# Two-layer encoder trunk on one core: the last four row blocks of the output projection kept back and multiplied token tile by token tile, with the second half's norm statistics taken from the additions' sums and a square pass

## The reference, cut to what matters

```python
branch = jnp.einsum('ble,ed->bld', y, w_out[i])          # 1024 x 2048 times 2048 x 1024
x = layer_norm(ALPHA * x + branch, ln_g[i], ln_b[i])     # mean and variance over 1024 features
```

## Time and profile before

| | us |
|---|---|
| three runs of before: median (lowest to highest) | 2169.07 (2167.77 to 2170.2) |
| the profiled execution, its own time | 2170.46 |
| its span, first to last instruction | 2168.6 |

### The profile page before, as it was taken

How to read it: one execution, slowest core, us unless ns; L and a number is a source line. 1 busy time by engine, 2 the same in 40 slices (tenths; PEclk the granted TensorE clock), 3 DMA queues, 4 the chain that set the end, 5 groups by cost and what they waited for, 6 DMA issues and landing times.

```text
span 2168.6 us, 31853 instructions
## 1 busy us (share of the span) xinstructions
PE 2107.2 (97%) x10880; PEld 1767.9 (82%) x10880; DVE 1628.4 (75%) x3673; ACT 1091.1 (50%) x2649; POOL 48.4 (2%) x65
## 2 busy tenths in 40 slices
PE   8999999999999995999999999999999999999996
PEld 8888888888888774888888888888888888888875
DVE  6777878787663568868888888888887888775485
ACT  5444444445553323455555555555555565564332
POOL 0000000000000021000000000000000000000031
PEclk9999999999999997999999999999999999999998
DMA  8311111111126542123233133133143233224643
GB/s 266 103 48 42 60 39 49 59 59 59 54 80 216 182 141 102 54 69 94 63 97 93 56 100 95 50 108 99 50 108 86 63 108 85 89 87 161 216 142 131
DMA packets 244619, 209.20 MB, mean 96 GB/s; under 512 B 21092, under 2 KB 198316, under 8 KB 244460
## 3 DMA queue, kind: packets, MB, share of 16 engines
q1 hardware_dynamic: 244460, 207.16, 31.8%
HBM read 172.60 MB, written 34.52 MB: 96 GB/s over the span
## 4 chain that ended last, share of the span: by engine, by line
PE 78%; DVE 13%; DMA 5%; issue 2%; ACT 2%; SPq 0%; DVEq 0%; ACTq 0%
PE bank L1086 15%; PE bank L1084 15%; PE bank L1085 15%; PE bank L1162 8%; PE bank L1134 7%; DVE work L1536 5%; PE bank L1256 4%; PE bank L1260 4%; PE bank L1262 4%; PE bank L1148 4%; DVE ring L1536 2%; DMA work<-weight_scratch 1%; DMA weight_scratch<-trig 1%; DVE x_ops L1536 1%; PE bank L1063 1%
## 5 line engine op out<-in xcount | busy, mean ns | idle before, releaser
L1084 PE MATMUL bank<-x_ops,ring 128*128 128x512 f32 (+1 forms) x1808 | 844.5, 467 | 16.9 <-issue 14.8
L1086 PE MATMUL bank<-x_ops,ring 128*128 128x512 f32 (+1 forms) x1808 | 698.9, 387 | 0.0
L1085 PE MATMUL bank<-x_ops,ring 128*128 128x512 f32 (+1 forms) x1808 | 697.0, 386 | 0.0
L1536 DVE SCALAR_TENSOR_TENSOR ring<-raw,ring 128x512 fp32r<-128x512 f32 x400 | 272.9, 684 | 232.9 <-ACT ring L1302 232.6
L1086 PEld LDWEIGHTS bank<-x_ops,ring 128*128 128x128 f32 x1808 | 341.0, 189 | 71.3
L1084 PEld LDWEIGHTS bank<-x_ops,ring 128*128 128x128 f32 x1808 | 345.7, 191 | 61.4 <-issue 15.5
L1363 ACT COPY work<-bank 128x256 f32<-128x256 f32 (+2 forms) x448 | 164.3, 367 | 430.1 <-PE bank L1148 429.3
L1085 PEld LDWEIGHTS bank<-x_ops,ring 128*128 128x128 f32 x1808 | 345.5, 191 | 37.5
L1302 ACT CAST ring<-raw 128x512 fp32r<-128x512 f32 x400 | 246.5, 618 | 198.4 <-PE bank L1262 173.0
L1162 PEld LDWEIGHTS bank<-work 128*128 128x128 f32 x1744 | 262.2, 190 | 44.4 <-ACT work L1363 3.9
L1380 ACT ACTIVATE work<-work,soft 128x256 f32<-128x256 f32 (+2 forms) x448 | 226.5, 506 | 134.3 <-DVE soft L1680 132.6
(11 more groups left out here) (74 smaller groups left out, 2020.8 us busy)
## 6 DMA issues: line engine op xcount, KB each, us to landing
raw<-in_w_in_b SPq DMA_DIRECT2D x160, 256.0 KB, 3.1
raw<-in_w_out SPq DMA_DIRECT2D x128, 256.0 KB, 2.9
raw<-in_w_in_a SPq DMA_DIRECT2D x80, 256.0 KB, 3.0
work<-weight_scratch SPq DMA_DIRECT2D x24, 768.0 KB, 5.2
y_scratch<-work SPq DMA_DIRECT2D x32, 512.0 KB, 2.8
x_ops<-y_scratch SPq DMA_DIRECT2D x64, 256.0 KB, 3.7
work<-v_scratch SPq DMA_DIRECT2D x48, 256.0 KB, 4.4
raw<-in_w_mkv SPq DMA_DIRECT2D x32, 256.0 KB, 5.1
```

What stands on the lines that cost most here:

```text
L1084: nc.tensor.matmul(dst, w_h, x_h, start=start, stop=False, skip_group_check=again)
L1085: nc.tensor.matmul(dst, w_h, x_l, start=False, stop=False, skip_group_check=again)
L1086: return nc.tensor.matmul(dst, w_l, x_h, start=False, stop=stop, skip_group_check=again)
L1536: return nc.vector.scalar_tensor_tensor(out=dst, in0=a, scalar=1.0, in1=b, op0=ALU.mult, op1=op)
```

## The change

Row blocks 8 to 11 (`LATE`) lose their places in the sequence. In each half TensorE first goes over the other 12 blocks (`EARLY`) as before, and then, for each token tile t, over the four late blocks and both column halves: 24 matmuls that complete the two banks of tile t. So the banks of a half are complete tile by tile, 24 matmuls apart. For this the split weights of the late blocks (in the place of x operands 4 and 5) and their split y tiles stay in SBUF. The weights are loaded and split once per layer, in the first half, behind places 1, 4, 7 and 10 of the 12; a layer has 56 weight stages in place of 64. The late y tiles are loaded and split in both halves, at the same places. `y_raw` keeps its two slots.

The order of the DMA queue, ScalarE and VectorE is now by stages m. After a stage with c = 1 of an early block come its y tile and, at places 1, 4, 7, 10, the late block's. The residual rows of tiles 0 to 3 are loaded at places 5 to 8 of the first half, those of tiles 4 to 7 at places 1 to 4 of the second.

The second half's statistics: `accum_out` of the two additions gives the row sum, GpSimd makes minus the mean of it (two operations), ScalarE squares the shifted row and sums it (`squares`), GpSimd scales by 1/D and goes on as before; one multiplication by -1 is gone. `norm(t)` on VectorE now comes after the additions of tile t+1, not after all additions.

Layer 1's operand 0: its transposes are done on TensorE inside the last section of layer 0 (three groups after tile 2's matmuls, one after tile 3's), into banks 2 to 5. ScalarE casts three groups after `squares(7)` and the last after tile 7's normalisation, VectorE takes three groups before `norm(6)` and the last before `norm(7)`. The first two token sums of tile i follow `norm` of tile 4+i. The third and fourth token sums come after the differences of the same step, not before.

```diff
+EARLY = (0, 1, 2, 3, 4, 5, 6, 7, 12, 13, 14, 15)
+LATE = (8, 9, 10, 11)
+OUT_ORDER = []
+for half in range(2):
+    for place, block in enumerate(EARLY):
+        OUT_ORDER += [(half, block, 0), (half, block, 1)]
+        if half == 0 and place % 3 == 1:
+            OUT_ORDER += [(0, LATE[place // 3], 0), (0, LATE[place // 3], 1)]
+Y_ORDER = [(half, block) for half in range(2) for place, early in enumerate(EARLY)
+           for block in ((early, LATE[place // 3]) if place % 3 == 1 else (early,))]
...
+            def load_y(layer, q):
+                h, e = Y_ORDER[q]
+                if q >= 2:
+                    sp.wait_ge(y_lo, layer * 2 * NE + q - 1)
...
+                for m in range(AHEAD, OUT_STAGES + AHEAD):
+                    loads_after(OUT_STAGE[layer] + m)
+                    if m >= OUT_STAGES:
+                        continue
+                    h, e, c = OUT_ORDER[m]
+                    if c == 1 and e in EARLY:
+                        place = EARLY.index(e)
+                        if h == 0 and 5 <= place < 9:
+                            load_residual(layer, residual, place - 5)
+                        if h == 0 and place >= 10:
+                            load_norm(layer, place - 10)
+                        if h == 1 and 1 <= place < 5:
+                            load_residual(layer, residual, 3 + place)
+                    for q in y_events(m):
+                        if q + 1 < 2 * NE:
+                            load_y(layer, q + 1)
...
                 for h in range(2):
-                    for e in range(NE - 2):
+                    for e in EARLY:
                         is_split(h, e)
                         for b in range(8):
-                            add_to(h, e, b, first=e == 0, ends=b >= 6)
-                    last_two(h)
+                            add_to(h, e, b, first=e == EARLY[0], ends=b >= 6)
+                    for t in range(4):
+                        for e in LATE:
+                            if t == 0:
+                                is_split(h, e)
+                            for c in range(2):
+                                add_to(h, e, 2 * t + c, last=e == LATE[-1])
+                        if layer == 0 and h == 1 and t >= 2:
+                            for i in ((0, 1, 2), (3,))[t - 2]:
+                                x_group(1, 0, i)
...
+                for m in range(AHEAD, OUT_STAGES + AHEAD):
+                    if OUT_STAGE[layer] + m < STAGES:
+                        split_hi(OUT_STAGE[layer] + m)
+                    for q in y_events(m) if m < OUT_STAGES else ():
+                        y_tile(layer, q)
+                def squares(t):
+                    n = layer * 4 + t - 3
+                    act.wait_ge(ln_sum, 2 * n)
+                    nc.scalar.activation(squared, rows[:, t, :], ACT.Square, bias=mv[:, t, 0:1],
+                                         accum_out=mv[:, t, 1:2]).then_inc(ln_square, 1)
+                squares(4)
                 for t in range(4, TILES):
-                    act.wait_ge(ln_mean, 2 * (layer * 4 + t - 3))
+                    if layer == 0 and t == 7:
+                        for i in range(3):
+                            x_group(1, 0, i)
+                    act.wait_ge(ln_mean, layer * 4 + t - 3)
                     nc.scalar.activation(rows[:, t, :], rows[:, t, :], ACT.Identity,
                                          bias=rstd[:, t, 0:1], scale=rstd[:, t, 1:2]
                                          ).then_inc(ln_normal[1], 1)
+                    if t + 1 < TILES:
+                        squares(t + 1)
+                if layer == 0:
+                    x_group(1, 0, 3)
...
+                second = 2 * NE + AHEAD
+                for m in range(AHEAD, second):
+                    stage(m)
+                for t in range(4):
+                    add(0, 2 * t)
+                    add(0, 2 * t + 1)
+                    statistics(t)
+                for m in range(second, OUT_STAGES + AHEAD):
+                    stage(m)
+                    if m in range(second + 8, second + 16, 2):
+                        norm((m - second - 8) // 2)
+                if layer == 0:
                     third_sum(FIRST_PAIR[1])
                     fourth_sum(FIRST_PAIR[1])
+                for i in range(4):
+                    add(1, 2 * i)
+                    add(1, 2 * i + 1)
+                    if layer == 0 and i == 3:
+                        for k in range(3):
+                            x_group(1, 0, k)
+                    if i > 0:
+                        norm(3 + i)
+                        if layer == 0:
+                            token_sums(1, i - 1)
+                            second_token_sums(1, i - 1)
+                if layer == 0:
+                    x_group(1, 0, 3)
+                norm(7)
+                if layer == 0:
+                    token_sums(1, 3)
+                    second_token_sums(1, 3)
```

More of the change, by code:

```diff
@@ L946, in run @@
                     store_outputs(layer, T)
[L947 to L950, removed]
+                    if T == products(layer) - 11:
+                        sp.wait_ge(*product_done(FIRST_PAIR[layer] + PAIRS[layer] - 1, 3))
+                        for q in range(2):
+                            load_y(layer, q)
@@ new lines, in load_y, with load_residual @@
+            def load_y(layer, q):
+                h, e = Y_ORDER[q]
+                if q >= 2:
+                    sp.wait_ge(y_lo, layer * 2 * NE + q - 1)
+                if h == 0:
+                    sp.wait_ge(*store_done[layer, e])
+                nc.sync.dma_start(y_raw[:, q % 2, :], y_dram[e, :, h * HALF:(h + 1) * HALF]
+                                  ).then_inc(y_full[q % 2], 16)
+            def load_residual(layer, residual, t):
+                if t == 0:
+                    for name in stored:
+                        if stores_after[layer][name]:
+                            sp.wait_ge(stored[name], 16 * stores_after[layer][name])
+                    if layer == 1:
+                        sp.wait_ge(rows_out, 16 * TILES)
+                nc.sync.dma_start(rows[:, t, :], residual[:, t, :]).then_inc(res_in[t], 16)
@@ L1097, in product_begins @@
                         pe.wait_ge(mv_free, DEPTH * MEM_HEADS)
[L1098 to L1099 removed]
+                    if j < 2 and layer == 1:
+                        pe.wait_ge(z_free, 8 + BRANCH_BANKS.index(j) + 1)
                 if j == 0 and not first:
@@ L1786, in run @@
                     if T < STEPS and T % 4 == 0:
+                        for op in X_BEFORE[layer][T // 4]:
+                            for i in range(4):
+                                x_group(layer, op, i)
                         if layer == 1 and T in (4, 8):
@@ L1917, in out_projection @@
-                for q in range(NE, 2 * NE - 1):
-                    stage_pair(q)
-                    if q < NE + 4:
-                        statistics(q - NE)
-                    elif q < NE + 8:
-                        norm(q - NE - 4)
-                n = OUT_STAGE[layer] + 4 * NE - 2
-                for b in range(8):
-                    add(1, b)
-                    if b % 2 == 1:
-                        statistics(4 + b // 2)
-                    if b == 2 and n + AHEAD < STAGES:
-                        split_lo(n + AHEAD)
@@ L1932, in out_projection @@
+                if layer == 0:
                     third_sum(FIRST_PAIR[1])
                     fourth_sum(FIRST_PAIR[1])
-                for t in range(4, TILES):
-                    norm(t)
+                for i in range(4):
+                    add(1, 2 * i)
[8 more added lines that the diff above has]
+                            second_token_sums(1, i - 1)
```

261 lines of the change are left out of this document (117 added, 144 removed).

## The result

| | median us | lowest to highest | against the kernel before |
|---|---|---|---|
| kernel before, beside it | 2169.77 | 2167.77 to 2171.97 (6 runs) | |
| changed kernel | 2184.74 | 2181.52 to 2192.89 (6 runs) | 1.0072 [1.006, 1.0083] |

What follows compares the result with a forecast made beforehand. The prediction took TensorE, busy 97% of the span, to bound the kernel. Between the layers -14.6, the end -5.5 and the y chain +24.3 gave +4.2 us: forecast 2174 us, range 2159 to 2185.

Steps and rivals of the forecast that it cites:

- What bounds the kernel: TensorE, busy 97% of the span; gains only where it stands still, between the layers and at the end; output projection reordered.
- Between the layers: From layer 0's last projection matmul (E) to layer 1's product 2: earlier products save 14.6 us, bounds -11 and -17.
- The end: After layer 1's last projection matmul: shorter VectorE tail saves 5.5 us, bounds -3.5 and -6.5; statistics' move about 1 of it.
- The waits of the y chain: In both output projections, late y tiles loaded only when wanted make TensorE wait 15.7 us per layer, against 5.1 and 4.0.
- The meeting at place 7: Second half of each projection: late tile, a norm and GpSimd's hold on VectorE coincide, making TensorE wait 5.5 us.
- the slow clock in the y chain's term: Slow matmuls after the 5.5 us wait in each projection: 1 us added per layer, between 0 and 2.
- the list: The prediction's waits place by place in the projections: 6.6 us in the first half, 9.1 in the second, per layer.
- 1 (late tiles land in time): Projections: late y loads land under 3.8 us on average, no wait at places 4, 7, 10; total 2157 to 2163; chance 0.20.
- 2 (no meeting at place 7): Projections' second half: VectorE catches up between norms, the rest holds; about 10 us less, 2165; chance 0.20.
- 3: Projections: waits feed on each other, landings near 6 us, the clock falls; +34, about 2186 us; chance 0.10.
- 4 (no overlap): Between the layers: product 0 behind norm(7) or GpSimd's slow chain, only -11 us; no chance of its own.
- The sum: Whole kernel: -14.6 - 5.5 + 24.3 = +4.2 us, forecast 2174 us; chance 0.50.

Runs made afterwards that it cites:

- second profile: The changed kernel itself run once more, unedited, for another profile: median 2185.65 us, span 2181.9 us.
- e2_norm_moved: Changed kernel with the four norms beside the second half's blocks moved apart, to places 5, 6, 8 and 9, so none falls at place 7: 2177.57 us.
- e1_deep: Changed kernel with four slots in place of two for raw y tiles, each loaded three events ahead: 2142.26 us, ratio 0.9869 to the kernel before.
- e5_three: Changed kernel with three slots for raw y tiles, each loaded two events ahead: 2146.74 us, ratio 0.9888 to the kernel before.
- e4_vecb: Changed kernel with the second half's bias additions of residual tiles 0 to 3 on VectorE in place of GpSimd: 2179.06 us.

## Why the prediction was right and wrong

- **What bounds the kernel**: right. Both gaps and the projections moved, and little else.
- **Between the layers, -14.6**: right, a little small. Product 0 at E+9.55 (forecast +9.8), product 1 at +19.2 (+19.5), product 2 at +23.7 (+25.2). With the 1.4 us of transposes inside the projection the term measured -16.1; the 1.5 us beyond the forecast lie between products 1 and 2, for which I kept the 5.7 us of the kernel before where 4.5 were measured.
- **The end, -5.5**: right, -5.7 at E+11.9 (forecast +12.0). The share of the statistics was 0.55, not 1.
- **The waits of the y chain**: right in place, and in size as a sum. Forecast 15.7 per layer; measured 16.7 and 16.1, and 14.8 and 15.3 in the second profile. That the sum came so near is partly luck: first half 8.8 and 9.2 in the first profile (forecast 6.6), second half 7.8 and 6.9 (forecast 9.1), errors of opposite sign. The meeting at place 7 gave 5.0, 4.25, 4.4 and 4.3 us (forecast 5.5; the forecast's own times, 11.8 less 5.9, give 5.9), and it fell to 0 and 1.0 when the norms were moved (e2_norm_moved). That the late issue is the cause is shown by e1_deep and e5_three. The Trainium skill, "DMA: Bandwidth & Descriptors" (the rules for kernel authors), asks to issue early and wait late; the two runs agree: with the landings still at 4.7 and 4.5 us, 30.0 us of waits went to none and to 2.2.
- **The step that failed is the slow clock in the y chain's term.** The prediction added 1 us a layer, for the wait of 5.5 us alone, between 0 and 2. Measured: 1.7 and 6.3, and 6.3 and 4.3 us. Summed over both layers the term is 34.2 us in the first profile: waits 32.8, slow stretches 7.9, 2.6 small, less the 9.1 of the kernel before; in the second 30.1 + 10.6 + 2.3 - 9.1 = 33.9. Forecast: 31.4 + 2 - 9.1 = 24.3. (About half of the small part is the second matmul behind each wait, which starts 0.31 us after the first in place of 0.23, at either clock and in the kernel before too; the rest I have not assigned.) So the clock is 5.9 of the 9.9 us that the term lacked in the first profile, the waits 1.4 and the small part 2.6; in the second the clock is 8.6, the small part 2.3, and the waits 1.3 less than forecast, together 9.6.
- **Why it was mis-sized**: I priced one slow stretch of 1 us per layer, behind the longest wait. The two profiles of the changed kernel show one of 1.5 to 1.7 us (once 2.7) behind 11 of the 12 waits of 2.0 us or more, and none behind the 21 shorter ones. The rows I had (product 1's 0.78 behind a longer gap) showed that matmuls slow down behind a gap, not how short a wait can be that does it. And waits spread: in the first profile the list's 1.6, 1.9, 1.5 and about 1 came out at up to 2.9, 2.4, 2.1 and 2.6.
- **Rivals**: 1 (late tiles land in time) was wrong: the late tiles' loads landed in 4.6 and 4.5 us on average in the two profiles, above the 3.8 at which I let it decide. 2 (no meeting at place 7) was wrong. 3 gave the right size, +34, by half the mechanism, so in part by luck: the clock fell, but landings stayed at a median of 4.7 and the waits did not grow beyond the list. 4 (no overlap) was wrong.
- **The sum**: forecast +4.2; spans +17.6 and +13.3. In the first, the chain's error is +9.9, between the layers -1.5, the end -0.2, the untouched body +4.7 and the start +0.6: 13.5, the difference. The second profile has +1.3 and -0.3 for body and start, and +13.3 in all; the medians, 15 us apart, lie between the two.

What decides whether a wait is followed by a slow stretch was not tried. That early loads take waits and slow matmuls away together (in e1_deep the projections have one delay of 0.2 us each) is shown.

## What to carry to other kernels

A load that is issued by the same event that makes it needed has no lead, and on an in-order engine its full landing time falls on everything queued behind it: count, per tile, how many events lie between issue and use, and give a kept operand its own slot. Here two more small slots turned a loss of 0.7% into a gain of 1.3%, with as many bytes and landings just as slow. When you price waits of TensorE, price the slow matmuls behind them as well, not only behind the longest: here some 1.6 us behind nearly every wait of 3 us or more and behind about half of those between 2 and 3.

## What was not expected of the hardware

The clock can fall after the work has resumed. Behind the 4.25 us wait of layer 1 the first matmuls run at full speed for 1.3 us, and then nine start 0.43 us apart (the last 0.39):

```profile
2128.90 0.47 PE L1330 MATMUL bank<-ring,x_ops 128*128 128x512 f32 x1 [4.09 <-DVE x_ops L1618]
2129.20 0.40 PE L1331 MATMUL bank<-ring,x_ops 128*128 128x512 f32 x1
...
2130.18 0.63 PE L1332 MATMUL bank<-ring,x_ops 128*128 128x512 f32 x1
...
2133.55 0.40 PE L1331 MATMUL bank<-ring,x_ops 128*128 128x512 f32 x1
```

The Trainium skill, "TensorE: Matmul & The Clock Gate" (the part on the clock gate), says that the gate follows how busy TensorE has lately been and has two levels; the trace agrees with both (0.50 and 1.00). It also puts the penalty of the ramp, the first matmuls that run at the lower level, under 1% of a typical kernel span. Here all slow stretches inside the projections are 7.9 of 2186 us and 10.6 of 2182, under 0.5%, and yet more than half of what the forecast of this term lacked.

Waits of the same length were not treated alike: one of 2.43 us (layer 0, first profile) left the clock alone, in e4_vecb four of the six between 2.0 and 2.9 did, and in e2_norm_moved one of 3.34 did while one of 1.98 did not. And the y tiles' loads landed at a median of 4.4 to 4.8 us in the kernels with the change, lead of one or three events alike, against 3.7 in the two without; what makes that 1 us was not taken apart.
